# The second attention's first chunks on the residual not yet normed, and two sums of squares in one pass

## The reference, cut to what matters

```python
def rmsnorm(x, g):
    y = xf * lax.rsqrt(jnp.mean(xf * xf, axis=-1, keepdims=True) + EPS)
    return (y * g)

# end of the first model
x = x + (jax.nn.silu(gate) * val) @ w_down[l]
return rmsnorm(x, final_norm_g)

# start of the second model
h = rms_norm(x, norm_mix) * (1 + sc_m) + sh_m        # modulate
qkv = (h @ w_qkv)                                    # 1024 -> 3 x 8 heads x 128
q = rms_norm(q, q_gain) * 128 ** -0.5 ;  k = rms_norm(k, k_gain)
# attention over the blocks (one block of 256 here, causal), then @ w_o, times g_m, plus x
```

## Time and profile before

| | |
|---|---|
| median of 3 runs | 915.56 us (915.34 to 915.65) |
| the profiled execution's own time | 915.08 us |
| its span in the trace | 913.1 us |
| TensorE busy | 901.0 us (99%) |
| VectorE busy | 749.8 us (82%) |
| ScalarE busy | 503.2 us (55%) |
| granted TensorE clock, mean | 1.00 |

### The profile page before, as it was taken

How to read it: one execution, slowest core, us unless ns; L and a number is a source line. 1 busy time by engine, 2 the same in 40 slices (tenths; PEclk the granted TensorE clock), 3 DMA queues, 4 the chain that set the end, 5 groups by cost and what they waited for, 6 DMA issues and landing times.

```text
span 913.1 us, 18258 instructions
## 1 busy us (share of the span) xinstructions
PE 901.0 (99%) x7367; PEld 876.0 (96%) x7367; DVE 749.8 (82%) x1032; ACT 503.2 (55%) x775; POOL 49.7 (5%) x87
## 2 busy tenths in 40 slices
PE   8999999999999989999999999999999999999998
PEld 7999999999999979999999999999999999999786
DVE  6989989989989789897988887977998887667444
ACT  6446757666664457664664454435644564444531
POOL 5100000000001000010000100100000000000000
PEclk9999999999999999999999999999999999999999
DMA  9887475656559837576469988874587467765541
GB/s 296 274 291 257 130 245 192 219 184 230 191 224 349 298 116 257 182 253 201 136 196 319 329 306 332 318 262 160 189 295 256 139 221 250 243 210 181 184 139 47
DMA packets 132128, 207.71 MB, mean 227 GB/s; under 512 B 4710, under 2 KB 109536, under 8 KB 126944
## 3 DMA queue, kind: packets, MB, share of 16 engines
q1 hardware_dynamic: 123968, 156.47, 51.1%
q0 software_dynamic: 8064, 50.34, 15.8%
q10 hardware_dynamic: 32, 0.01, 0.0%
HBM read 205.75 MB, written 1.05 MB: 226 GB/s over the span
## 4 chain that ended last, share of the span: by engine, by line
PE 92%; DVE 5%; ACT 1%; issue 1%; DMA 1%; SPq 0%; DVEq 0%; ACTq 0%
PE bank L1671 26%; PE bank L1672 25%; PE bank L1673 25%; PE bank L1823 2%; PE bank L1740 2%; PE bank L1742 2%; PE bank L1751 2%; PE bank L1716 1%; DVE w_lo L1000 1%; PE bank L1708 1%; PE bank L1710 1%; ACT w_hi L583 1%; DMA x_in<-in_x 1%; PE bank L2068 0%; PE bank L2067 0%
## 5 line engine op out<-in xcount | busy, mean ns | idle before, releaser
L1000 DVE TENSOR_TENSOR w_lo<-w_raw,w_hi 128x1024 fp32r<-128x1024 f32 x294 | 354.0, 1221 | 109.8 <-ACT w_hi L583 108.5
L583 ACT ACTIVATE w_hi<-w_raw 128x1024 fp32r<-128x1024 f32 x294 | 307.2, 1056 | 244.9 <-PE bank L1673 229.9
L1671 PE MATMUL bank<-act_hi,w_hi 128*128 128x256 f32 x1312 | 365.9, 279 | 0.1
L1672 PE MATMUL bank<-act_lo,w_hi 128*128 128x256 f32 x1312 | 362.7, 276 | 0.0
L1673 PE MATMUL bank<-act_hi,w_lo 128*128 128x256 f32 x1312 | 362.7, 276 | 0.0
L1671 PEld LDWEIGHTS bank<-act_hi,w_hi 128*128 128x128 f32 x1312 | 246.4, 188 | 0.7 <-issue 0.6
L1672 PEld LDWEIGHTS bank<-act_lo,w_hi 128*128 128x128 f32 x1312 | 246.5, 188 | 0.4 <-issue 0.2
L1673 PEld LDWEIGHTS bank<-act_hi,w_lo 128*128 128x128 f32 x1312 | 246.4, 188 | 0.0
L1016 DVE SCALAR_TENSOR_TENSOR ada_acc<-ada_raw,silu_c,ada_acc 128x2048 f32<-128x2048 f32 (+1 forms) x56 | 114.3, 2040 | 1.8 <-DMA ada_raw<-in_w_ada 1.5
L1671 PE MATMUL bank<-hid_hi,w_hi 128*128 128x256 f32 x352 | 98.3, 279 | 0.0
L1672 PE MATMUL bank<-hid_lo,w_hi 128*128 128x256 f32 x352 | 97.3, 277 | 0.0
(11 more groups left out here) (307 smaller groups left out, 1373.6 us busy)
## 6 DMA issues: line engine op xcount, KB each, us to landing
w_raw<-in_w_gate_up SPq DMA_DIRECT2D x44, 1024.0 KB, 5.2
ada_raw<-in_w_ada POOLq DMA_DIRECT2D x40, 1024.0 KB, 5.3
w_raw<-in_w_down SPq DMA_DIRECT2D x33, 1024.0 KB, 5.6
w_raw<-in_w_in SPq DMA_DIRECT2D x23, 1024.0 KB, 7.0
w_raw<-in_w_up SPq DMA_DIRECT2D x22, 1024.0 KB, 5.3
w_raw<-in_w_qkv SPq DMA_DIRECT2D x12, 1024.0 KB, 7.0
w_raw<-in_w_out SPq DMA_DIRECT2D x8, 1024.0 KB, 6.5
ada_raw<-in_w_ada POOLq DMA_DIRECT2D x16, 512.0 KB, 4.7
```

The costliest lines, as they stand in the source:

```text
L583: act.activation(unit(w_hi, u), raw_half(c, h), ACT.Copy).then_inc(hi_ready, 1)
L1000: dve.tensor_tensor(unit(w_lo, u), raw_half(c, h), unit(w_hi, u).bitcast(F32), ALU.subtract).then_inc(lo_ready, 1)
L1671: pe.matmul(dst, a_hi, b_hi, start=start, stop=False, skip_group_check=True)
L1672: pe.matmul(dst, a_hi, b_lo, start=False, stop=False, skip_group_check=True)
```

## The change

- Norm 2 is raw as well: RAW_INDEX takes it in, `raw_hi`/`raw_lo` copies for it lie in a place of their own (`rawq`), and chunks 0 and 1 of the second attention are `raw_chunk`s, into banks 4, 5 and 6, 3. VectorE gets the eight `raw_lower` products in the down layer, ScalarE the eight `raw_upper` copies.
- Both sums of squares come from one pass: `both_gain` now holds ones in its first 64 columns and the squared gain in the other 64, so the plain sum lands on partitions 0 to 63 of the bank and the weighted one on 64 to 127. `final_sums` goes. What reads the sums (logarithm and mean, for both norms) does so in two instructions of 64 partitions each.
- The banks of chunks 0 and 1 must be scaled before anything reads them: VectorE's new `raw_heads(b)` does it, `head_squares` of these two waits for it (`qk_scaled`), and adds the shift by its bias.
- The order changes: norm 2 is called with c0=QKV, which puts four weight splits of VectorE into it; the splits of c = 0 go from the loops. `head_rms(0)` stands at (1, 1) behind `head_squares(1)`, `head_norm(0)` and the final mean at (2, 0), `final_scale` at (2, 1), the residual's scaling at c = 3 to 6 instead of 2 to 5, and the first three of ADA_AT2 at (3, 1), (4, 1), (5, 1) instead of (0, 0), (2, 0), (5, 0).
- On TensorE the `head_sums` of chunk c - 1 stand where they stood, in the first half of c; since chunk 1 is now issued whole in its first half, `head_sums(0)` comes behind it.

```diff
-ADA_AT2 = [(0, 0), (2, 0), (5, 0), (7, 0), (8, 0), (10, 0)]
+ADA_AT2 = [(3, 1), (4, 1), (5, 1), (7, 0), (8, 0), (10, 0)]
-RAW_INDEX = {1: 0, 3: 1, 4: 2, 5: 3}
+RAW_INDEX = {n: n - 1 for n in range(1, 6)}
+HEAD_RAW = ((4, 5), (6, 3))
...
 # ScalarE
             def norm(n, shift=None, c0=None):
 
+                act.wait_ge(ss_ready, n)
                 if n == 2:
                     act.wait_ge(eps2_set, 1)
-                act.wait_ge(ss_ready, n)
-                act.activation(n_y[:], bank[SUM_BANK[n]][:, 0:T], ACT.Ln, bias=eps2[:] if n == 2 else eps[:],
-                               scale=1.0 / D).then_inc(ln_ready, 1)
+                    for half in range(2):
+                        ins = act.activation(n_y[64 * half:64 * half + 64, :], bank[SUM_BANK[n]][64:P, 0:T], ACT.Ln,
+                                             bias=eps2[64:P, :], scale=1.0 / D)
+                else:
+                    ins = act.activation(n_y[:], bank[SUM_BANK[n]][:, 0:T], ACT.Ln, bias=eps[:], scale=1.0 / D)
+                ins.then_inc(ln_ready, 1)
...
-                if n == 4:
+                if n % 2 == 0:
                     split_unit(c0 + 1, 0)
...
-                        act.activation(both_gain[:, k, :], ones[:], ACT.Identity, bias=eps[:], scale=final_sq[:, k:k + 1]
-                                       ).then_inc(both_ready, 1)
+                        act.activation(both_gain[:, k, 0:64], ones[:, 0:64], ACT.Copy)
+                        act.activation(both_gain[:, k, 64:P], ones[:, 64:P], ACT.Identity, bias=eps[:],
+                                       scale=final_sq[:, k:k + 1]).then_inc(both_ready, 1)
...
             def head_squares(n):
 
+                dst = (k2, q2)[n % 2][:, 2 * (n // 2):2 * (n // 2) + 2, :]
+                if n:
+                    act.wait_ge(qk_ss, n)
+                if n < 2:
+                    act.wait_ge(qk_scaled, n + 1)
+                    for t in range(2):
+                        src, shift = bank[HEAD_RAW[n][t]][:, 0:T], raw_shift[:, 2 * n + t:2 * n + t + 1]
+                        act.activation(h_sq[:, t * T:(t + 1) * T], src, ACT.Square, bias=shift)
+                        ins = act.activation(dst[:, t, :], src, ACT.Identity, bias=shift)
+                    ins.then_inc(qk_sq, 1)
+                    return
...
             for c in range(15):
                 for h in range(2):
+                    if (c, h) == (0, 1):
+                        final_logs()
                     if h == 1 and c in QK_AT:
                         head_squares(QK_AT.index(c))
-                    split_unit(QKV + c + 2, h)
-                    if h == 0 and c - 1 in QK_AT:
+                    if (c, h) == (1, 1):
+                        head_rms(0)
+                    if c:
+                        split_unit(QKV + c + 2, h)
+                    if h == 0 and c > 1 and c - 1 in QK_AT:
                         head_rms(QK_AT.index(c - 1))
                     attend2(c, h)
...
 # VectorE
-            norm(2, lambda k: both2[:, k:k + 1], 2, shift=lambda k: mod[:, 0, SH_M + k:SH_M + k + 1])
-            split_unit(QKV + 1, 1)
-            final_scale()
+            norm(2, lambda k: first_gain(2, k), 2, shift=lambda k: mod[:, 0, SH_M + k:SH_M + k + 1], c0=QKV)
+
+            def raw_heads(b):
+
+                dve.wait_ge(unit_done, 2 * (QKV + b) + 2)
+                for t in range(2):
+                    ins = dve.tensor_copy(raw_shift[:, 2 * b + t:2 * b + t + 1], bank[HEAD_RAW[b][t]][:, T:T + 1])
+                link(ins)
+                for t in range(2):
+                    src = bank[HEAD_RAW[b][t]][:, 0:T]
+                    ins = dve.tensor_tensor(src, src, rstd[:], ALU.mult)
+                ins.then_inc(qk_scaled, 1)
+            raw_heads(0)
...
             for c in range(14):
                 for h in range(2):
-                    if h == 1 and c - 1 in QK_AT:
+                    if (c, h) == (1, 1):
+                        raw_heads(1)
+                    if h == 1 and c > 1 and c - 1 in QK_AT:
                         head_norm(QK_AT.index(c - 1))
+                    if (c, h) == (2, 1):
+                        final_scale()
...
-                    split_unit(QKV + c + 2, h)
+                    if c:
+                        split_unit(QKV + c + 2, h)
+                    if (c, h) == (2, 0):
+                        final_mean()
+                        head_norm(0)
                     attend2(c, h)
-                    if 2 <= c < 6:
-                        final_residual(2 * (c - 2) + h)
+                    if 3 <= c < 7:
+                        final_residual(2 * (c - 3) + h)
...
 # TensorE
             down_layer(DOWN1, 0)
-            square_rest(2, 2)
             pe.wait_ge(mod_done, 2)
-            final_sums()
...
             for c in range(16):
-                if 2 <= c < 12:
+                if 4 <= c < 12:
                     if c - 2 in QK_AT:
...
                 for h in range(2):
-                    if c == 0:
+                    if c < 2:
                         if h == 0:
-                            chunk(QKV, bank[0], act_hi, act_lo, operand=2)
+                            raw_chunk(QKV + c, c, 2, c == 0)
                     elif c < 12:
-                        half_chunk(QKV + c, h, bank[c % 2], act_hi, act_lo, moving=c in V_AT)
+                        half_chunk(QKV + c, h, bank[c % 2], act_hi, act_lo, operand=2 if c == 2 else None,
+                                   moving=c in V_AT)
                     else:
                         out2_chunk(c - 12, h)
                     if h == 0 and c - 1 in QK_AT:
```

More of the change, by code:

```diff
@@ L41 @@
 SUM_BANK = (2, 6, 2, 6, 2, 6)
-FINAL_BANK = 3
 EPS2 = EPS * EPS
@@ L328, in model_kernel @@
         qk_ss = sem("qk_ss")
+        qk_scaled = sem("qk_scaled")
         qk_a = sem("qk_a")
@@ L405, in first_gain @@
                 return vcol(0, V_FFN + k)
+            if n == 2:
+                return both2[:, k:k + 1]
             return gain2[:, n - 2, k:k + 1]
@@ L608, in squares @@
                 if raw:
-                    for k in range(5 if n == 4 else 6, KT):
+                    for k in range(6 if n % 2 else 5, KT):
                         raw_upper(n, k)
@@ L887, in _, with final_logs @@
             squares(2, 2, (QKV + 1, 0), 2)
-            norm(2, shift=lambda k: mod[:, 0, SH_M + k:SH_M + k + 1])
-            split_unit(QKV + 1, 1)
-            act.wait_ge(final_ss, 4)
-            act.activation(f_y[:], bank[FINAL_BANK][:, 0:T], ACT.Ln, bias=eps[:], scale=1.0 / D).then_inc(final_ln, 1)
-            act.wait_ge(final_ln, 1)
-            act.activation(f_y[:], f_y[:], ACT.Exp, scale=-0.5).then_inc(final_y, 1)
-            def head_squares(n):
+            norm(2, shift=lambda k: mod[:, 0, SH_M + k:SH_M + k + 1], c0=QKV)
+            def final_logs():
+                for half in range(2):
+                    ins = act.activation(f_y[64 * half:64 * half + 64, :], bank[SUM_BANK[2]][0:64, 0:T], ACT.Ln,
+                                         bias=eps[0:64, :], scale=1.0 / D)
+                ins.then_inc(final_ln, 1)
+                act.wait_ge(final_ln, 1)
+                act.activation(f_y[:], f_y[:], ACT.Exp, scale=-0.5).then_inc(final_y, 1)
+            def head_squares(n):
+                dst = (k2, q2)[n % 2][:, 2 * (n // 2):2 * (n // 2) + 2, :]
[9 more added lines that the diff above has]
+                    return
                 act.wait_ge(unit_done, 2 * (QKV + QK_AT[n]) + 2)
                 src = bank[QK_AT[n] % 2][:, :]
-                if n:
-                    act.wait_ge(qk_ss, n)
                 act.activation(h_sq[:], src, ACT.Square)
-                dst = (k2, q2)[n % 2][:, 2 * (n // 2):2 * (n // 2) + 2, :]
                 act.activation(dst, src.rearrange("p (t n) -> p t n", n=T), ACT.Copy).then_inc(qk_sq, 1)
@@ L1021, in norm @@
                 dve.wait_ge(ln_ready, n)
-                link(dve.tensor_scalar(n_a[:], bank[SUM_BANK[n]][:, 0:T], -0.5 / D, -0.5 * (EPS2 if n == 2 else EPS),
-                                       ALU.mult, ALU.add))
+                if n == 2:
+                    for half in range(2):
+                        ins = dve.tensor_scalar(n_a[64 * half:64 * half + 64, :], bank[SUM_BANK[n]][64:P, 0:T], -0.5 / D,
+                                                -0.5 * EPS2, ALU.mult, ALU.add)
+                else:
+                    ins = dve.tensor_scalar(n_a[:], bank[SUM_BANK[n]][:, 0:T], -0.5 / D, -0.5 * EPS, ALU.mult, ALU.add)
+                link(ins)
                 dve.wait_ge(y_ready, n)
@@ L1525, in _, with final_mean @@
             down_layer(DOWN1, None)
[L1526 to L1529 removed]
+            norm(2, lambda k: first_gain(2, k), 2, shift=lambda k: mod[:, 0, SH_M + k:SH_M + k + 1], c0=QKV)
[3 more added lines that the diff above has]
+                    ins = dve.tensor_copy(raw_shift[:, 2 * b + t:2 * b + t + 1], bank[HEAD_RAW[b][t]][:, T:T + 1])
+                link(ins)
+                for t in range(2):
```

(12 more changed lines are left out.)

42 lines of the change are left out of this document (21 added, 21 removed).

## The result

The changed kernel takes 930.7 us (median of 4, 929.44 to 931.49); the kernel before, on the same chip, 915.61. The ratio is 1.0155, 95% interval 1.0139 to 1.0172. The forecast was 928.6 in a range from 920 to 932. The profiled execution took 931.45 us, its span is 929.8; the other three took 931.49, 929.94 and 929.44.

A forecast was written before the change was run, and what follows sets the result against it. TensorE, busy for 99% of the span, bounds the kernel, with VectorE nearly full in this stage. TensorE's second head sum 5.3 us late plus further backlog of 8 us gave +13.0 us: 928.6 us, range 920.0 to 932.0.

The forecast's parts named there:

- The sum: Whole kernel: +13.0 us on the profiled run's 915.08 us, median 928.6 us.
- the first squares' extra delay: At the seam before the second attention: one product moved ahead of the update lengthens TensorE's 2.0 us wait by 0.2.
- the halved logarithm and mean: In norm 2, each done twice on 64 partitions: 0.8 us together, so rstd ends at 333.8.
- norm(2) from rstd to the scaling: On VectorE, four weight splits, eight products and eight lower parts before the first scaling: 11.0 us, finished at 344.8.
- raw_heads(0): VectorE's scaling of chunk 0's banks behind norm 2: 1.05 us with the hand-over, done at 345.9.
- head_squares(0): ScalarE's four instructions behind raw_heads(0), awaited by the first head sum: 1.55 us, done at 347.4.
- the first wait: TensorE stands still between chunk 1 and head_sums(0), from 340.6 to 347.4: 6.8 us.
- VectorE's hole: VectorE idle near 5 us behind raw_heads(1), from 350.6 to 355.8, ending with a weight split.
- the part on the backlog: VectorE's lag makes the sixth head sum 13.1 us late; TensorE loses a further 8 us in waits at chunks 4 to 7.
- First and fourth shift: VectorE's scores' shifts in the second attention: first at 365.2, 8.1 us late; fourth at 394.4, 29.2 us after.
- the low clock behind the long wait: If TensorE returned at 1.2 GHz, head_sums(0) and half of chunk 2 cost 3.6 us more; the 1.2 us lag is hidden.
- The second wait: TensorE ahead of head_sums(1): waits 2.4 us, starting at 353.4 where it was 348.11, 5.3 us late.

The follow-up runs named there:

- the early scaling: Changed kernel with chunk 0's banks scaled ahead of norm 2's products on VectorE, and their head squares ahead of ScalarE's upper parts: 928.91 us, ratio 1.0132.
- the three products: Changed kernel with the three modulation (ada) products it had moved to c = 3, 4, 5 put into VectorE's two idle times: 926.07 us, ratio 1.0108.
- the two sums in one pass: Kernel before with only the one-pass sums of squares, read in halves of 64 partitions; chunks 0 and 1 still wait for the norm: 917.93 us, ratio 1.0027.
- the filling: Changed kernel with 14 idle constant matmuls behind chunk 1 on TensorE: 930.71 us. Also 13 on a kernel with modulation products behind c = 7: 919.65 against 921.85 us.
- The products back at their old places: Changed kernel with its first three modulation (ada) products back at (0,0), (2,0), (5,0): 929.81 us, ratio 1.0146.
- the splits: Changed kernel with ScalarE's two weight splits of c = 1 put ahead of head_squares(0) and head_squares(1): 927.5 us, ratio 1.0122.
- no holes: Changed kernel with seam product moved, early scaling, earlier ScalarE splits, raw_heads(1) directly behind norm 2 and one modulation product at (1, 1): 924.41 us, ratio 1.0088.

## Why the prediction was right

**The sum and the cause.** +13.0 us were forecast, and the medians are 15.1 apart. The spans of the two profiled runs are 16.7 apart, 3.7 more than forecast: 0.7 for the later start, 1.5 for the low clock at the seam, 0.5 between the seam and the sixth head sum (13.5 with the 0.2 at the squares), and 1.0 behind it. The first of these is chance; that the sum of them stayed inside the range, 1.3 us from its upper end, is in part luck. The chain by its steps, forecast first: the first squares' extra delay 0.2 (0.2 measured); the halved logarithm and mean 0.8 (0.9: two means of 64 partitions took 0.87 where one of 128 takes 0.42, and the ScalarE pair 0.95 where one logarithm takes 0.47); norm(2) from rstd to the scaling 11.0 (11.0); raw_heads(0) 1.05 (347.14 to 348.17); head_squares(0) 1.55 (348.20 to 349.76); the first wait 6.8 (6.3, as chunks 0 and 1 took 13.97 us and not 13.33, with 0.24 of waiting for a lower part in them, while the chain from the start of chunk 0 to the head sum took 20.3 for 20.1); VectorE's hole about 5 (5.12). In the last steps the prediction's own sums are loose: 397.8 against 384.44 is 13.4, or 13.2 without the overlap, and it says 13.1 and then 13.0. The experiments with the early scaling and with the three products show that the lag is VectorE's, as the part on the backlog had it: a wait of TensorE that was taken away came back at the next head sum, and work taken out of VectorE's full stretch shortened it nearly by its own length.

**First and fourth shift.** Forecast at 365.2 and 394.4, measured 367.46 and 396.68. Both are 2.3 us behind the forecast, which is the later start (0.7) and the clock at the seam (1.5); the 29.2 us between them came as forecast.

**The missing term.** "The granted clock is 1.00 (2.4 GHz) in every window, also in that with 2.0 us of idle time", I wrote, and so expected no drop from a wait of 2.2. Behind it the clock was 0.58, and 1.5 us went there, the largest single term of the 3.7 us. I had one profiled run at clock 1.000 to go by; seven of 17 runs of that kernel have another. Nor does every such wait bring the clock down: behind 2.49 us in the trace with the three products, and behind 2.3 us at the seam in that with the two sums in one pass, it stayed at 1.00. Of the second place the forecast was right: the low clock behind the long wait "would be hidden", as the first scores wait for VectorE. The Trainium skill, TensorE: Matmul & The Clock Gate, Part 1, has idling as what puts the clock down; the traces agree in that it fell behind waits of 2.2, 4.6 and 6.3 us, and they also have waits of 2.0 to 2.5 us behind which it did not.

**The second wait.** Forecast at 2.4 us for a head sum at 353.4. In the changed kernel it doesn't show, because at half speed TensorE itself comes at 356.13; with the filling it shows, 2.1 us.

**Where single expectations failed.** The products back at their old places gained 0.9 us and not 4; the splits 2 to 3 and not 3.6; no holes 924.4 and not 921.5. In the last two I took an idle time to be a fixed store of time, but it is the distance to another engine's hand-over, and shrinks or comes back elsewhere when one end is moved. In the first the idle time was filled as expected, and the waits in the later stretch were not hidden.

## What to carry over

Before a norm is taken out of the path by scaling afterwards, ask where the scaling stands in its engine's queue: here it stood behind the whole of the norm that it was to replace, on an engine that was 98% busy in that stage. Matmuls that are saved in the shadow of a chain save nothing. And a small wait of TensorE at a seam is worth more than its length if the clock can fall behind it: the best kernel of this study is the one before with a single product moved, 913.35 us.

## What the runs showed of the hardware

- An instruction on 64 partitions lasts as long as one on 128: 0.87 us for two means of 64x256, of which one of 128x256 took 0.42 before the third mixer, and two logarithms of 64x256 take 0.95 on ScalarE where one of 128x256 takes 0.47. The cycle table of the Trainium skill, VectorE: DVE Perf Modes, "The TRN2 errata", counts elements of the free dimension only, and the traces agree.
- TensorE's clock fell to about half (0.50 to 0.61 in the windows, some of which hold a little at full clock; that is the 1.2 GHz level) after waits of 2.2, 4.6, 5.9 and 6.3 us. It did not fall at the seam after 2.0 us in the profiled run of the kernel before, after 2.3 with the two sums in one pass, and after 2.5 with the three products in idle time. So at 2 to 2.5 us it is open from one execution to the next. Where it falls, the squares take 2.05 us for four matmuls instead of 1.10.
- The filling products of two constants, 5.8 to 6.2 us of them, kept it at 1.00.
- A mean clock of 1.00 does not mean that TensorE is at its full pace: three of the fourteen profiled executions have 510 or 511 matmuls between 655 and 715 us where the kernel before has 529, and lose 2.1 us by it. The cause stays open.
